# Gated-delta inverse: masks applied as products leave PSUM, blocks gathered and returned by copies with three whole transposes, gate projections regrouped

## The chip, the cores and the metric

One core of a Trainium2 chip runs the whole program once. The time is device microseconds (us) of that execution. TensorE is called PE below, VectorE DVE, ScalarE ACT, GpSimd POOL, the DMA-issuing SyncE SP.

## What is computed

Two blocks of transformer layers on 256 tokens of width 1024, in float32. The first block has two layers (L = 0, 1); each has one input projection, three mixers (state-space, latent attention, gated delta rule), gates and a feed-forward part. The change lies in the gated delta rule, which solves a triangular system per chunk and head:

```python
a_mat = jnp.where(strict, jnp.einsum('bhcld,bhcmd->bhclm', kb, k) * decay, 0.0)
rhs = jnp.concatenate([v * beta[..., None], kb * jnp.exp(g)[..., None]], axis=-1)
sol = lax.linalg.triangular_solve(a_mat + jnp.eye(L, dtype=jnp.float32), rhs, left_side=True, lower=True)
u, w = jnp.split(sol, [DV], axis=-1)
```

The kernel uses chunks of 128 tokens: 2 chunks x 8 heads = 16 triangular matrices of 128x128, each of which it inverts.

## The kernel before

**Streams and order.** Every engine walks the same list of turns (`order1` for a layer of the first block). A turn names a stream (a projection such as `gate_g`, `gate_s`, `xbc`, or a mixer such as `gdn`) and how many of its steps come next; each engine emits its own part of the step. So the list fixes the order on all engines. What PE does in the fill turns covers what the other engines do for `gdn`.

**Projections.** A turn of `gate_g`, `gate_s`, `z`, `lat` or `xbc` is one group of 48 matmuls on PE (lines 912 to 914) from two chunks of weights. A weight chunk arrives by a DMA from SP into a ring of three slots (each two chunks, 1 MB), ACT rounds it to its high part (line 1469, `prepare`), and DVE (line 2103) or POOL (line 2931) subtracts to get the low part; `by_pool` in `rings` picks which. A high slot is free only once PE has used the chunk two groups earlier, so ACT makes the highs of the next group right after the last group ended. For the gate projections ACT then evicts the group (line 1561). `ada0` is a turn of 16 small matmuls (line 871) with a DVE addition (lines 2121, 2124).

**The inverse** (`gdn`, in each engine's class). PE turns (line 837) and ACT negates (line 1772) the 16 matrices into `K.AT`. Then:
- DVE gathers the 16x16 diagonal blocks with four transposes of 32 partitions each (line 2439), puts them into `W` by two predicated copies (line 2444) and inverts them all at once with 28 small operations (`solved`, lines 2432 and 2434). ACT spreads the result (line 1786, four activations) and DVE returns it with eight transposes of 32 partitions (line 2452), four for `K.X`, four for `K.XT`.
- `LEVELS` joins blocks of 16 to 32, 64 and 128, in 12 steps (three levels x four groups of four matrices). A step: POOL masks `AT` into `BT` (line 3022), PE multiplies it by `X` ("y", line 1123), ACT evicts to `Y` (line 1797), PE multiplies by `XT` ("j", line 1131), DVE adds to `XT` (line 2462), PE turns that (line 837) and ACT copies it to `X` (line 1778). On PE, step n is y of the next step, j of this one, the turning of the last one.

Of the kernel before, what the change touches and what calls it, by code (L numbers as in the profile page):

```python
# [153 lines left out]
class Shared:  # L154
# [90 lines left out]
    def rings(self):  # L245
# [3 lines left out]
        for p, (mat, _, c) in enumerate(self.plan()):  # L249
# [4 lines left out]
            self.hi_of[p], self.hi_before[p], self.by_pool[p] = h, at.get(h), mat == "win" and (c < 28 or 52 <= c < 56)  # L254
# [143 lines left out]
    def block1_memory(self):  # L398
# [20 lines left out]
        self.turned, self.W, self.tmp16 = small[:, 0:512], blocks(small[:, 512:768], 16), small[:, 768:832]  # L419
        self.spread = [small[:, 1024 + 512 * i:1536 + 512 * i] for i in range(2)]  # L420
# [135 lines left out]
def order1(L):  # L556
# [18 lines left out]
    yield from [("gdn", 1), ("xbc", 2), ("lat", 1), ("xbc", 1), ("lat", 1), ("gdn", None), ("ssd", 1)]  # L575
# [244 lines left out]
class TensorE(Engine):  # L820
# [243 lines left out]
    def gdn(self, L):  # L1064
# [44 lines left out]
        yield  # L1109
# [8 lines left out]
        def below(lev, q):  # L1118
            P = self.open("gd_y", L, lev, q)
            self.wait_ge(*at("gd_g", "mask", L, lev, q))  # L1120
            self.wait_ge(*(at("gd_s", "X", L, lev - 1, q) if lev > 4 else at("gd_v", "X16", L)))
            for j in range(4):
                i = mm(bank(P, j), K.BT[:, 4 * q + j, :], K.X[:, 4 * q + j, :], True, True)
            i.then_inc(*up("gd_p", "y", L, lev, q))

        def joined(lev, q):
            P = self.open("gd_j", L, lev, q)
            self.wait_ge(*at("gd_s", "Y", L, lev, q))
            self.wait_ge(*(at("gd_v", "XT", L, lev - 1, q) if lev > 4 else at("gd_v", "XT16", L)))
# [326 lines left out]
class ScalarE(Engine):  # L1456
# [291 lines left out]
    def gdn(self, L):  # L1748
# [21 lines left out]
        for c, g in CG:  # L1770
            self.wait_ge(*at("gd_p", "u", L, c, g))
            self.act(K.AT[:, 8 * c + 4 * g:8 * c + 4 * g + 4, :], four(self.bank("gd_u", L, c, g)), ACT.Copy, scale=-1.0).then_inc(*up("gd_s", "A", L, c, g))
            self.emptied("gd_s", "gd_u", L, c, g)
        yield
# [18 lines left out]
        def below(lev, q):  # L1793
# [1449 lines left out]
```

## Time and profile before

| | us |
|---|---|
| median of 3 runs | 2610.51 (2609.53 to 2613.84) |
| the profiled execution | 2610.93 |
| its span | 2609.1 |
| PE busy in the span | 2515.6 (96%) |
| DVE, ACT, POOL busy | 1465.1, 1255.3, 363.5 |

The execution's own time is 1.8 us above its span and 0.4 us above the median of the runs. In the profile, "idle before <-releaser" names what ended an engine's wait, and PEclk is the granted TensorE clock as a share of full speed.

### The profile page before, as it was taken

The numbers are of one execution on the slowest core, as the hardware profiler recorded it, in microseconds if no ns is written. First come the engines' busy times: TensorE is split into PE (matmuls) and PEld (weight loads), VectorE is DVE, ScalarE is ACT, GpSimd is POOL, SyncE is SP. The second block draws the span as 40 slices with busy tenths as digits, with TensorE's granted clock in tenths as the row PEclk, the third lists the DMA queues.
The fourth block names the chain that finished last, engine by engine and source line by source line (L and its number), as shares of the span: only waits on it lengthen the run. The fifth ranks groups of instructions, "written<-read, shape, count | busy, mean of one in ns | idle before, by whom it ended". The sixth has DMA issues, their size and how long they took to land.

```text
span 2609.1 us, 44133 instructions
## 1 busy us (share of the span) xinstructions
PE 2515.6 (96%) x19246; PEld 2326.1 (89%) x19246; DVE 1465.1 (56%) x2212; ACT 1255.3 (48%) x1856; POOL 363.5 (14%) x211
## 2 busy tenths in 40 slices
PE   7989999999999899999999999999999999999999
PEld 7979988999999799979999886787779998888999
DVE  4762865665357547756666337553334554676654
ACT  6635554454366365545644267542223453334442
POOL 5144000000153240000001004300000001331000
PEclk9989999999999899999999999999999999999999
DMA  5334444455543344435554336233334552113455
GB/s 182 131 114 162 146 152 155 162 178 189 185 140 135 114 162 146 162 130 194 175 181 146 109 105 223 82 129 130 145 116 171 199 170 88 67 64 126 165 182 174
DMA packets 56016, 383.90 MB, mean 147 GB/s; under 512 B 6032, under 2 KB 9744, under 8 KB 10000
## 3 DMA queue, kind: packets, MB, share of 16 engines
q1 hardware_dynamic: 55104, 375.90, 41.8%
q10 hardware_dynamic: 720, 5.18, 0.5%
q8 instruction: 152, 2.49, 0.4%
q14 instruction: 40, 0.33, 0.0%
HBM read 380.01 MB, written 1.05 MB: 146 GB/s over the span
## 4 chain that ended last, share of the span: by engine, by line
PE 82%; DVE 10%; ACT 4%; DMA 2%; issue 1%; POOL 0%; DVEq 0%; ACTq 0%; POOLq 0%
PE ps L912 20%; PE ps L914 20%; PE ps L913 20%; DVE r L2103 3%; PE ps L1411 1%; PE ps L1039 1%; PE ps L871 1%; ACT r L1469 1%; PE ps L991 1%; PE ps L993 1%; PE ps L992 1%; PE ps L950 1%; PE ps L951 1%; PE ps L952 1%; PE ps L1131 1%
## 5 line engine op out<-in xcount | busy, mean ns | idle before, releaser
L912 PE MATMUL ps<-r,r 128*128 128x256 f32 (+1 forms) x4512 | 1345.7, 298 | 17.8 <-DVE r L2103 12.2
L914 PE MATMUL ps<-r,r 128*128 128x256 f32 (+1 forms) x4512 | 1332.5, 295 | 0.0
L913 PE MATMUL ps<-r,r 128*128 128x256 f32 (+1 forms) x4512 | 1332.4, 295 | 0.0
L2103 DVE TENSOR_TENSOR r<-ring,r 128x1024 fp32r<-128x1024 f32 (+2 forms) x550 | 668.8, 1250 | 554.8 <-ACT r L1469 554.5
L912 PEld LDWEIGHTS ps<-r,r 128*128 128x128 f32 x4512 | 852.9, 189 | 52.0 <-issue 15.2
L914 PEld LDWEIGHTS ps<-r,r 128*128 128x128 f32 x4512 | 852.3, 189 | 25.0
L913 PEld LDWEIGHTS ps<-r,r 128*128 128x128 f32 x4512 | 852.4, 189 | 24.0 <-issue 0.5
L1469 ACT ACTIVATE r<-ring 128x1024 fp32r<-128x1024 f32 (+1 forms) x614 | 612.5, 1039 | 307.6 <-DMA ring<-in_fi 68.8
L2982 POOL TENSOR_TENSOR slab<-slab 128x512 f32<-128x512 f32 (+1 forms) x20 | 28.7, 1434 | 1296.5 <-ACT slab L1589 1276.1
L2931 POOL TENSOR_TENSOR r<-ring,r 128x1024 fp32r<-128x1024 f32 x64 | 152.5, 2407 | 157.0 <-ACT r L1469 146.8
L2194 DVE SCALAR_TENSOR_TENSOR slab<-ps,v,slab 128x255 f32<-128x255 f32 (+1 forms) x168 | 67.5, 473 | 73.6 <-ACT slab L1541 73.6
L991 PE MATMUL ps<-r,r 128*128 128x256 f32 (+2 forms) x304 | 89.2, 294 | 0.5 <-DVE r L2103 0.4
L992 PE MATMUL ps<-r,r 128*128 128x256 f32 (+2 forms) x304 | 87.4, 288 | 0.0
L993 PE MATMUL ps<-r,r 128*128 128x256 f32 (+2 forms) x304 | 87.4, 287 | 0.0
L950 PE MATMUL ps<-r,r 128*128 128x256 f32 x240 | 72.3, 301 | 10.0 <-DVE r L2278 7.7
L3039 POOL TENSOR_TENSOR slab<-slab,posi 128x1024 f32<-128x1024 f32 (+1 forms) x32 | 46.9, 1468 | 220.8 <-DVE posi L2761 220.8
L1561 ACT ACTIVATE slab<-ps 128x512 f32<-128x512 f32 x48 | 28.5, 594 | 92.8 <-PE ps L914 92.6
L951 PE MATMUL ps<-r,r 128*128 128x256 f32 x240 | 70.2, 292 | 0.0
L952 PE MATMUL ps<-r,r 128*128 128x256 f32 x240 | 70.0, 292 | 0.0
L1610 ACT ACTIVATE r<-slab 128x512 fp32r<-128x512 f32 x33 | 20.8, 632 | 98.4 <-DVE slab L2260 98.4
L3067 POOL TENSOR_TENSOR slab<-slab 128x512 f32<-128x512 f32 x32 | 50.4, 1574 | 102.2 <-PE ps L1411 84.2
L1589 ACT ACTIVATE slab<-x 128x512 f32<-128x512 f32 x36 | 22.7, 631 | 85.7 <-DVE x L2236 52.0
(328 smaller groups left out, 2836.7 us busy)
## 6 DMA issues: line engine op xcount, KB each, us to landing
ring<-in_win SPq DMA_DIRECT2D x76, 1024.0 KB, 4.9
ring<-in_ada SPq DMA_DIRECT2D x48, 1024.0 KB, 4.9
ring<-in_fi SPq DMA_DIRECT2D x44, 1024.0 KB, 4.8
ring<-in_fo SPq DMA_DIRECT2D x36, 1024.0 KB, 4.8
ring<-in_wup SPq DMA_DIRECT2D x32, 1024.0 KB, 4.9
ring<-in_wdn SPq DMA_DIRECT2D x32, 1024.0 KB, 4.8
ring<-in_hin SPq DMA_DIRECT2D x20, 1024.0 KB, 4.8
ring<-in_nqkv SPq DMA_DIRECT2D x12, 1024.0 KB, 4.7
```

The lines of the kernel that those rows point to most:

```text
L912: self.mm(o, hi[:, k - k0, cs], xh, k == 0, False)
L913: self.mm(o, hi[:, k - k0, cs], xl, False, False)
L914: i = self.mm(o, lo[:, k - k0, cs], xh, False, k == last)
L950: self.mm(o, hi, xh, k == 0 and t % per == 0, False, skip_group_check=True)
L951: self.mm(o, hi, xl, False, False, skip_group_check=True)
L952: i = self.mm(o, lo, xh, False, k == kt - 1, skip_group_check=True)
L991: self.mm(o, xh, cut(hi, k), k == 0, False)
L992: self.mm(o, xh, cut(lo, k), False, False)
L993: i = self.mm(o, xl, cut(hi, k), False, k == kt - 1)
L1469: self.act(K.high(p), K.raw(p), ACT.Copy).then_inc(*self.up("w_hi", p))
L2103: self.tt(K.low(p), K.raw(p), K.high(p).bitcast(F32), ALU.subtract).then_inc(*self.up("w_lo_v", p))
L2931: self.tt(K.low(p), K.raw(p), K.high(p).bitcast(F32), ALU.subtract).then_inc(*self.up("w_lo_g", p))
```

## The change

1. `rings`: the low parts of the first four chunks of `gate_s` (52 to 55), two groups, are made by DVE instead of POOL.
2. Gathering: ACT and DVE each copy two of the four diagonal 32-partition strips into one tile, and one transpose of all 128 partitions follows. Return: ACT and DVE each spread one half, one whole transpose for `X` and one for `XT`, and then copies of the strips, two by ACT and two by DVE.
3. Masks: POOL's masking of `AT` is gone. PE multiplies the unmasked `AT`, and DVE multiplies the product by the (transposed) mask as it leaves PSUM; ACT no longer evicts it.
4. `order1`: one more `gate_s` group stands before the first level, one empty step of `gdn` is gone, and an `xbc` turn takes the place of the `gate_s` turn after the levels.
5. A table load before the second half of the output norm is left out, and buffers move.

```diff
@@ rings
-            self.hi_of[p], self.hi_before[p], self.by_pool[p] = h, at.get(h), mat == "win" and (c < 28 or 52 <= c < 56)
+            self.hi_of[p], self.hi_before[p], self.by_pool[p] = h, at.get(h), mat == "win" and c < 28
@@ order1
-    yield from [("gdn", 1), ("gate_g", 1), ("gdn", 1), ("gate_g", 1), ("gdn", 1), ("gate_s", 1), ("gdn", 1), ("gate_s", 1),
-                ("gdn", 1), ("ada0", 1)]
+    yield from [("gdn", 1), ("gate_g", 1), ("gdn", 1), ("gate_g", 1), ("gate_s", 1), ("gdn", 1), ("gate_s", 1),
+                ("gdn", 1), ("gate_s", 1), ("ada0", 1)]
     for _ in range(3):
         yield from [("gdn", 4), ("ada0", 1)]
-    yield from [("gate_s", 1), ("gdn", 1), ("gate_s", 1)]
+    yield from [("gate_s", 1), ("gdn", 1), ("xbc", 1)]
...
-    yield from [("gdn", 1), ("xbc", 2), ("lat", 1), ("xbc", 1), ("lat", 1), ("gdn", None), ("ssd", 1)]
+    yield from [("gdn", 1), ("xbc", 1), ("lat", 1), ("xbc", 1), ("lat", 1), ("gdn", None), ("ssd", 1)]
@@ TensorE.gdn
        def below(lev, q):
-            self.wait_ge(*at("gd_g", "mask", L, lev, q))
-            self.wait_ge(*(at("gd_s", "X", L, lev - 1, q) if lev > 4 else at("gd_v", "X16", L)))
+            if lev > 4:
+                self.wait_ge(*at("gd_s", "X", L, lev - 1, q))
+            else:
+                self.wait_ge(*at("gd_s", "X16", L, 0))
+                self.wait_ge(*at("gd_v", "X16", L, 0))
-                i = mm(bank(P, j), K.BT[:, 4 * q + j, :], K.X[:, 4 * q + j, :], True, True)
+                i = mm(bank(P, j), K.AT[:, 4 * q + j, :], K.X[:, 4 * q + j, :], True, True)
        def joined(lev, q):
-            self.wait_ge(*at("gd_s", "Y", L, lev, q))
+            self.wait_ge(*at("gd_v", "Y", L, lev, q))
@@ ScalarE.gdn
+        for a in quarter[:2]:
+            m = self.act(K.small[a, :].rearrange("p (t x m) -> p t x m", t=16, x=2), K.AT[a, :, a].rearrange("p m (x t) -> p t x m", x=2), ACT.Copy)
...
-            for x in range(2):
-                self.wait_ge(*at("gd_v", "W", L, 14))
-                m = self.act(K.spread[i].rearrange("p (i x m) -> p i x m", i=16, x=2)[:, :, x, :], K.W.rearrange(order), ACT.Copy,
-                             scale=K.upper[x][:, 0, 1:2])
+            self.wait_ge(*at("gd_v", "W", L, 14))
+            self.act(K.spread[i].rearrange("p (i x m) -> p i x m", i=16, x=2)[:, :, 0, :], K.W.rearrange(order), ACT.Copy,
+                     scale=K.upper[0][:, 0, 1:2]).then_inc(*up("gd_s", "spread", L, i))
+        for i, dst in enumerate((K.X, K.XT)):
+            self.wait_ge(*at("gd_v", "back", L, i))
+            for a in quarter[:2]:
+                m = self.act(dst[a, :, a].rearrange("p m (x i) -> p i x m", x=2), K.back[i][a, :].rearrange("p (i x m) -> p i x m", i=16, x=2), ACT.Copy)
-        def below(lev, q):
-            self.act(K.Y[:, 4 * q:4 * q + 4, :], four(self.bank("gd_y", L, lev, q)), ACT.Copy).then_inc(*up("gd_s", "Y", L, lev, q))
@@ VectorE.gdn
-        for a in quarter:
-            self.e.transpose(K.turned[a, :].rearrange("p (t x m) -> p t x m", t=16, x=2),
-                             K.AT[a, :, a].rearrange("p m (x t) -> p t x m", x=2)).then_inc(*up("gd_v"))
+        for a in quarter[2:]:
+            self.e.tensor_copy(K.small[a, :].rearrange("p (t x m) -> p t x m", t=16, x=2), K.AT[a, :, a].rearrange("p m (x t) -> p t x m", x=2)).then_inc(*up("gd_v"))
+        self.e.transpose(K.turned, K.small).then_inc(*up("gd_v"))
...
+        def back(i, order, dst):
+            self.ts(K.spread[i].rearrange("p (i x m) -> p i x m", i=16, x=2)[:, :, 1, :], W.rearrange(order), K.upper[1][:, 0, 1:2], None, ALU.mult).then_inc(*up("gd_v"))
+            self.wait_ge(*at("gd_s", "spread", L, i))
+            self.e.transpose(K.back[i], K.spread[i]).then_inc(*up("gd_v", "back", L, i))
+            for a in quarter[2:]:
+                self.e.tensor_copy(dst[a, :, a].rearrange("p m (x i) -> p i x m", x=2),
+                                   K.back[i][a, :].rearrange("p (i x m) -> p i x m", i=16, x=2)).then_inc(*up("gd_v"))
...
+        def below(lev, q):
+            self.tt(K.Y[:, 4 * q:4 * q + 4, :], four(self.bank("gd_y", L, lev, q)), bc(K.C[f"t{lev}"].unsqueeze(1), [128, 4, 128]),
+                    ALU.mult).then_inc(*up("gd_v", "Y", L, lev, q))
@@ PoolE.gdn
-        def below(lev, q):
-            self.tt(K.BT[:, s4, :], K.AT[:, s4, :], mask(f"t{lev}"), ALU.mult).then_inc(*up("gd_g", "mask", L, lev, q))
```

How instructions now stand. In the changed kernel DVE's lines 2112, 2428, 2441 and 2443 are 2103, 2419, 2432 and 2434 of the kernel before, and ACT's 1478, 1570, 1782 are 1469, 1561, 1772. `r_52` and `r_53` are the two slots of highs, `r_49` to `r_51` the lows.

DVE before, from the last `gdn` step ahead of the inverse to its first operations:

```order
L2419 TENSOR_TENSOR slab<-ps,slab 128x512 x4
L2103 TENSOR_TENSOR r_50<-ring,r_52 128x1024 x2
L2439 STREAM_TRANSPOSE slab<-slab 32x512 x4
L2444 COPY_PREDICATED slab<-cst,slab 128x256 x2
L2432 TENSOR_TENSOR slab<-slab 128x14
```

DVE of the changed kernel at the same place:

```order
L2428 TENSOR_TENSOR slab<-ps,slab 128x512 x4
L2112 TENSOR_TENSOR r_50<-ring,r_52 128x1024 x2
L2112 TENSOR_TENSOR r_51<-ring,r_53 128x1024 x2
L2112 TENSOR_TENSOR r_49<-ring,r_52 128x1024 x2
L2448 COPY slab<-slab 32x512 x2
L2451 STREAM_TRANSPOSE slab<-slab 128x512
L2455 COPY_PREDICATED slab<-cst,slab 128x256 x2
L2441 TENSOR_TENSOR slab<-slab 128x14
```

Two pairs of lows (for the first and second `gate_s` groups) now stand ahead of the gathering; a third pair stands in the middle of the 28 small operations.

ACT of the changed kernel, from the negation to the first turned blocks (before, it was negation, highs in `r_53`, eviction, highs in `r_52`, eviction, then the four activations of line 1786 and an eviction):

```order
L1782 ACTIVATE slab<-ps 128x512 x4
L1788 ACTIVATE slab<-slab 32x512 x2
L1478 ACTIVATE r_53<-ring 128x1024 x2
L1570 ACTIVATE slab<-ps 128x512
L1478 ACTIVATE r_52<-ring 128x1024 x2
L1570 ACTIVATE slab<-ps 128x512
L1478 ACTIVATE r_53<-ring 128x1024 x2
L1570 ACTIVATE slab<-ps 128x512
L1801 ACTIVATE slab<-slab,cst 128x16x16 x2
L1807 ACTIVATE slab<-slab 32x16x2x16 x4
L1570 ACTIVATE slab<-ps 128x512
```

The highs of the second `gate_s` group (`r_52`) stand behind the eviction of the last `gate_g` group, so DVE's second pair of lows, and with it the gathering, comes after that group's end on PE.

DVE of the changed kernel, from the return of `XT` to the first levels (the return of `X`, in the same three rows, stands ahead of it):

```order
L2461 TENSOR_SCALAR slab<-slab,cst 128x16x16
L2464 STREAM_TRANSPOSE slab<-slab 128x512
L2468 COPY slab<-slab 32x16x2x16 x2
L2130 COPY row<-ps 128x256
L2478 TENSOR_TENSOR slab<-ps,cst 128x512 x2
L2490 TENSOR_TENSOR slab<-slab,ps 128x512
L2478 TENSOR_TENSOR slab<-ps,cst 128x512
L2490 TENSOR_TENSOR slab<-slab,ps 128x512
```

The first masked product stands behind both returns and the `ada0` copy, and DVE has two operations per level step where it had one.

## Rows read from the trace of the kernel before

**Rows 1.** The page: busy time by engine, share of the span, instructions.
```profile
PE 2515.6 (96%) x19246; PEld 2326.1 (89%) x19246; DVE 1465.1 (56%) x2212; ACT 1255.3 (48%) x1856; POOL 363.5 (14%) x211
```
**Rows 2.** Waits of PE: engine line waited for, us in total, times, longest.
```profile
PE ps L1123 <- DVE slab L2452: 20.0, 2, 10.0
...
PE ps L1131 <- DVE slab L2452: 1.2, 2, 0.6
```
**Rows 3.** PE's timeline, layer 0: start, us, engine, line, operation, [idle before].
```profile
135.05 0.37 PE L912 MATMUL ps<-r,r 128*128 128x256 f32 x1
...
152.31 1.07 PE L871 MATMUL ps<-ring,silc 128*32 128x256 f32 x16
...
163.40 3.75 PE L1123 MATMUL ps<-slab 128*128 128x128 f32 x16 [10.01 <-DVE slab L2452]
...
173.06 1.06 PE L1123 MATMUL ps<-slab 128*128 128x128 f32 x8
173.96 1.06 PE L1131 MATMUL ps<-slab 128*128 128x128 f32 x8
...
191.91 1.06 PE L1131 MATMUL ps<-slab 128*128 128x128 f32 x8
```
**Rows 4.** PE's timeline, layer 1.
```profile
866.04 3.75 PE L1123 MATMUL ps<-slab 128*128 128x128 f32 x16 [10.03 <-DVE slab L2452]
...
875.95 1.06 PE L1123 MATMUL ps<-slab 128*128 128x128 f32 x8
```
**Rows 5.** Stretches: us of PE, PEld, DVE, ACT, POOL (count), then PEclk, DMA share.
```profile
88.00:90.00 2.00, 2.00 (x12) 2.00 (x11) 1.83 (x6) 0.00 (x0) 0.00 (x0) 0.50 0.00 0
...
165.00:170.00 5.00, 4.42 (x22) 4.16 (x21) 3.13 (x5) 1.20 (x2) 2.55 (x2) 0.50 0.00 0
...
716.00:718.00 2.00, 0.00 (x0) 0.00 (x0) 1.05 (x3) 1.42 (x4) 0.47 (x1) 1.00 0.07 23
```
**Rows 6.** DVE's timeline over the inverse, layer 0.
```profile
143.15 2.25 DVE L2432 TENSOR_TENSOR slab<-slab 128x14 f32<-128x14 f32 x1
...
154.76 0.22 DVE L2432 TENSOR_TENSOR slab<-slab 128x56 f32<-128x56 f32 x1
...
157.84 0.18 DVE L2434 TENSOR_TENSOR slab<-slab 128x14 f32<-128x14 f32 x1
159.00 8.58 DVE L2452 STREAM_TRANSPOSE slab<-slab 32x512 f32<-32x512 f32 x8 [0.97 <-ACT slab L1786]
```
**Rows 7.** POOL's timeline, the same stretch.
```profile
142.65 5.07 POOL L2931 TENSOR_TENSOR r<-ring,r 128x1024 fp32r<-128x1024 f32 x2 [0.73 <-ACT r L1469]
147.67 5.04 POOL L3022 TENSOR_TENSOR slab<-slab,cst 128x512 f32<-128x512 f32 x4
```
**Rows 8.** ACT's timeline, the same stretch.
```profile
141.03 0.60 ACT L1561 ACTIVATE slab<-ps 128x512 f32<-128x512 f32 x1 [3.00 <-PE ps L914]
141.53 2.00 ACT L1469 ACTIVATE r<-ring 128x1024 fp32r<-128x1024 f32 x2
146.72 0.60 ACT L1561 ACTIVATE slab<-ps 128x512 f32<-128x512 f32 x1 [3.20 <-PE ps L914]
```
**Rows 9.** Single lines: count, ns min/median/max.
```profile
L2444 DVE COPY_PREDICATED slab<-cst,slab x4: 647/1072/1496, 140.9 to 845.1; 128x256 f32<-128x256 int32 x4
L2522 DVE TENSOR_SCALAR slab<-slab x16: 426/427/428, 279.6 to 1017.1; 128x512 f32<-128x512 f32 x16
L2462 DVE TENSOR_TENSOR slab<-slab,ps x24: 403/687/689, 169.8 to 898.7; 128x512 f32<-128x512 f32 x16, 64x256 f32<-64x256 f32 x8
```
**Rows 10.** DVE's timeline in the third level, layer 0.
```profile
189.37 2.36 DVE L2103 TENSOR_TENSOR r<-ring,r 128x1024 fp32r<-128x1024 f32 x2 [1.32 <-ACT r L1469]
...
191.98 0.41 DVE L2462 TENSOR_TENSOR slab<-slab,ps 64x256 f32<-64x256 f32 x1
```
**Rows 11.** Two other waits of PE, in its timeline.
```profile
85.56 0.36 PE L912 MATMUL ps<-r,r 128*128 128x256 f32 x1 [2.75 <-DVE r L2103]
...
714.66 1.13 PE L1006 MATMUL ps<-slab,cst 128*128 128x256 f32 x4 [1.70 <-ACT slab L1589]
```

More of the change, by code:

```diff
@@ L418, in block1_memory @@
         small = self.y.rearrange("p a b -> p (a b)")
-        self.turned, self.W, self.tmp16 = small[:, 0:512], blocks(small[:, 512:768], 16), small[:, 768:832]
-        self.spread = [small[:, 1024 + 512 * i:1536 + 512 * i] for i in range(2)]
+        self.small, self.turned = small[:, 0:512], small[:, 512:1024]
+        sums = self.sq.rearrange("p a b -> p (a b)")
+        self.W, self.tmp16 = blocks(sums[:, 0:256], 16), sums[:, 256:320]
+        self.spread = [small[:, 1024 * i:1024 * i + 512] for i in range(2)]
+        self.back = [small[:, 512 + 1024 * i:1024 + 1024 * i] for i in range(2)]
         self.BT = self.rs.rearrange("p a (b c) -> p (a b) c", c=128)
@@ L1676, in squares, with logs @@
         self.act(sq, src, ACT.Square).then_inc(*self.up("n_s", "sq", pid))
-    def logs(self, pid, nt, per, n, inv, rs):
+    def logs(self, pid, nt, per, n, inv, rs, load=True):
         K, groups, pb = self.K, nt // per, 512 // n
-        self.e.preload_act_table_set(LN_EXP)
+        if load:
+            self.e.preload_act_table_set(LN_EXP)
         for g in range(0, groups, pb):
@@ L1773, in gdn @@
             self.emptied("gd_s", "gd_u", L, c, g)
+        quarter = [slice(32 * a, 32 * a + 32) for a in range(4)]
+        self.wait_ge(*mine("gd_s"))
+        for a in quarter[:2]:
+            m = self.act(K.small[a, :].rearrange("p (t x m) -> p t x m", t=16, x=2), K.AT[a, :, a].rearrange("p m (x t) -> p t x m", x=2), ACT.Copy)
+        m.then_inc(*up("gd_s", "small", L))
         yield
@@ L1831, in gdn @@
         for g in range(2):
-            self.logs(("go", L, g), 4, 1, T, 1 / 128, K.rs[:, 4 * g:4 * g + 4, :])
+            self.logs(("go", L, g), 4, 1, T, 1 / 128, K.rs[:, 4 * g:4 * g + 4, :], load=g == 0)
         for g in range(2):
@@ L2434, in solved @@
                 self.tt(W[:, 0:j, j + 1:16], W[:, 0:j, j + 1:16], t, ALU.add).then_inc(*up("gd_v", "W", L, j))
-        for a in quarter:
-            for c, g in CG:
-                self.wait_ge(*at("gd_s", "A", L, c, g))
-            self.e.transpose(K.turned[a, :].rearrange("p (t x m) -> p t x m", t=16, x=2),
-                             K.AT[a, :, a].rearrange("p m (x t) -> p t x m", x=2)).then_inc(*up("gd_v"))
+        for c, g in CG:
+            self.wait_ge(*at("gd_s", "A", L, c, g))
+        for a in quarter[2:]:
+            self.e.tensor_copy(K.small[a, :].rearrange("p (t x m) -> p t x m", t=16, x=2), K.AT[a, :, a].rearrange("p m (x t) -> p t x m", x=2)).then_inc(*up("gd_v"))
+        self.wait_ge(*mine("gd_v"))
+        self.wait_ge(*at("gd_s", "small", L))
+        self.e.transpose(K.turned, K.small).then_inc(*up("gd_v"))
         self.wait_ge(*at("gd_g", "W", L))
@@ L3011, in gdn @@
             self.e.memset(v, 0.0).then_inc(*up("gd_g", "zero", L, i))
[L3012 to L3028 removed]
+        yield
     def na(self):
```

54 lines of the change are left out of this document (22 added, 32 removed).

## The prediction

> **What bounds the kernel now.** I read the page first. PE is busy for 2515.6 of 2609.1 us [rows 1], so only what shortens PE's waits, or what it issues at a lowered clock, can show. The list of PE's waits comes next: two of about 10 us stand out, one in each layer, at the first product of the levels (line 1123), and both end with DVE's return transposes (line 2452); two more of 0.6 us follow at line 1131 [rows 2]. Then PE's timeline around them. In layer 0 PE starts the last `gate_g` group at 135.05, issues it, two `gate_s` groups and `ada0`, has nothing left at 163.40 - 10.01 = 153.39, and goes on at 163.40 [rows 3]; layer 1 shows the same with 10.03 [rows 4]. Last the stretches: the granted clock is 0.50, its 1.2 GHz level, from 165 to 170 with PE nearly always busy [rows 5]. The wait has lowered the clock for the work behind it.
>
> What this costs in all: at full clock a y or a j takes 173.96 - 173.06 = 0.90 us and the turning of four blocks, half as many matmul records, 0.45 by estimate; a step is 2.25. From 163.40 to 173.06 PE issues three y, two j and one turning, 5 x 0.90 + 0.45 = 4.95 at full clock, and takes 9.66 [rows 3]. With 0.58 of that a wait, 4.13 is clock. Layer 1: 875.95 - 866.04 = 9.91 [rows 4], so 4.38 is clock. Together 10.01 + 10.03 + 1.16 + 4.13 + 4.38 = **29.7 us**, the most that the change can win here.
>
> Why DVE is late: its first small operation of the inverse, on 14 elements, takes 2.25 us, and the last, of the same size, 0.18; from 154.76 on 14 of them take 3.26 together [rows 6]. The long ones lie beside POOL's lows and masks, which end at 152.71 [rows 7]. So DVE loses (154.76 - 143.15) - 3.26 = 8.35 us to them. The Trainium skill, SBUF - State Buffer, section "Who interferes with whom", says that a VectorE instruction with two SBUF inputs and a GpSimd instruction that reads SBUF lock each other out; by that rule the loss goes when POOL goes, and the trace agrees with 2.25 against 0.18.
>
> **The change, part by part (layer 0; layer 1 has the same offsets).**
>
> *Cover.* One more `gate_s` group now stands before the first y. A group takes 146.72 - 141.03 = 5.69 [rows 8]. PE is through at 153.39 + 5.69 = 159.08 if nothing stops it. The group is only moved, so its work costs nothing.
>
> *Start of DVE's chain.* DVE must make two pairs of lows before it gathers. The second pair's highs come after the last `gate_g` group: ACT starts them at 141.53 and takes 2.00 [rows 8], so DVE has the first at 142.6 and, at 2.36 for an undisturbed pair [rows 10], is free at 144.95. That is a loss: `AT` is there from about 136.
>
> *Gathering.* Two DVE copies of 32x512 (ACT's two run long before, from 136). The nearest rows: 0.43 for 512 elements by a scalar operation within SBUF, 0.69 out of PSUM [rows 9]; the strided side argues against the lower, so 0.55 each, 1.10. Even a strided strip can hardly exceed the 1.07 of a transpose of it (8.58 / 8) [rows 6]; the low end is 0.43. One transpose of 128x512: 1.07, the row of 32x512, because each partition has as many elements; ends 0.5 and, if strips were done one after another, 4.3. Two predicated copies at 0.65, the fastest seen (the slow 1.50 lay beside POOL) [rows 9]: 1.30. Sum 3.5: 148.45.
>
> *Inverse.* First 14 operations 3.3: 151.75. Then the third pair of lows, first at 152.95, both at 154.1. PE wants the first at 135.05 + 3 x 5.69 + 0.1 = 152.2, so it **waits 0.8** (through a gap that was covered by POOL before) and ends `ada0` (1.08, from 152.31 to 153.39 [rows 3]) at 159.85. Second 14 operations 3.3: 157.4.
>
> *Return.* Scaling on ACT, 0.6, beside DVE's, then the transpose 1.07: 159.15. ACT's two strips 1.2, DVE's 1.1: `X` at 160.45. PE **waits 0.6**. `XT`: DVE scaling 0.35, transpose 1.07, strips 1.1, with gaps 162.9. Then the `ada0` row 0.35 and the first masked product 0.69 (priced by an addition out of PSUM [rows 9]): 163.95. PE has issued two y by 162.25, so it **waits 1.75** for its first j.
>
> *Levels.* DVE now has 0.69 + 0.69 = 1.4 us per step of 2.25, and each masked product is asked for 1.3 us after its y ended. So PE keeps its pace, at one place excepted: in the third level DVE's lows end and its next operation starts at 191.98 [rows 10]. That is now a masked product, ready at about 192.75, and PE wants its j at 191.91 [rows 3]: it **waits 0.85**.
>
> *Costed at nothing:* the two `gate_s` pairs on DVE ahead of the gathering reach PE in time (the first at 139.6 for a group that begins at 140.8); POOL's freed time has no taker; ACT loses evictions and a table load, and PE waits for neither there; the `xbc` group in the place of the `gate_s` one is as long, and its lows (POOL, 4.8 us a pair) have the 5.69 of the `gate_s` group and the products behind the levels as cover. If that cover failed, at most a pair of lows, 4.8, would show. SP's transfers keep their order, only one group nearer.
>
> *Sum.* Waits left 0.8 + 0.6 + 1.75 + 0.85 = 4.0 a layer, 8.0 in all, so 29.7 - 8.0 = **21.7 us gained**, if the clock holds. The profiled execution would take 2610.93 - 21.7 = 2589.2; the median of the runs lies 0.4 lower, and I say 2589.
>
> **The rivals.**
>
> *The clock falls all the same.* A wait of 2.75 [rows 11] was followed by clock 0.50 [rows 5]; one of 1.70 [rows 11] left it at 1.00 even in the idle time after it [rows 5]. Here 0.6 and 1.75 stand 1.8 us apart: between the two. A fall costs between nothing and the 4.13 of now; behind waits a quarter as long I take 2 a layer: 2593. The Trainium skill, TensorE: Matmul & The Clock Gate, section "HAM oscillation", says that waits between bursts lower the clock again and the next burst starts slow; that rule gives this rival, and the trace bears it out for the 2.75 and not for the 1.70.
>
> *DVE's chain is shorter than PE's cover.* With copies at 0.43 and transposes at 0.5, the chain loses 0.7 + 1.1 before `XT` and more with ACT's part; all waits but that of the third level shrink under 1 us: 2582. For it: contiguous transposes. Against: the row.
>
> *Strips are slow.* Copies at 1.07 each: gathering +1.0, each return +1.0, so the waits grow by 3 to 4 a layer, and the clock falls: some 11 less gained: 2600.
>
> *A whole transpose is four strips long* (the other side). 4.3 instead of 1.07 is 3.2 more, three times: waits 0.8 + 0.6 + 1.75 + 0.85 + 9.6 = 13.6, and the clock falls twice as deep into the work, 4.3 as now and 2 behind the wait for the lows: 19.9 a layer against 14.9 now, 10 us slower: 2621 (2610.5 + 10). It decides from 1.6 us more per whole transpose, 2.7 in all. For it: no row has more than 32 partitions. Against: every other DVE row costs by elements per partition.
>
> *POOL was not the cause:* then the first small operations stay long, 8.4 a layer, and the waits with clock come to about 13 of 14.9: 2607. The two rows of one size speak against it.
>
> **How the numbers follow.** Forecast 50%; clock falls 25%; shorter chain 9%; slow strips 9%; long transposes 4%; POOL not the cause 3%. The predicted time is the forecast's, **2589**. From 2581 (all of the 29.7 gained) to 2600 the first four are taken in, with unnamed shifts of PE's phase of a few us. A measurement of this kernel tells about 0.2%, 5 us, from no change. Faster: the first four, 93%. Same: 3% from the last rival. Slower: 4%.
>
> **What would show it.** DVE's small operations all at 0.18 to 0.25 beside an idle POOL; the gathering copies starting near 145; a whole transpose at about 1.07; PE's waits at line 1123 and at the first j of about 0.6 and 1.75, one at the third `gate_s` group of 0.8, and PEclk at 1.00 through the levels. Wrong would be: a wait at line 1123 over 3 us, PE waiting at every j (then DVE's two operations per step are the bound), or `X` ready before PE is.

## The result

The changed kernel takes **2593.7 us**, the median of 4 runs (2591.63 to 2595.91), against 2610.02 (2607.0 to 2613.84) for the kernel before on the same chip: ratio 0.9937, 95% interval 0.992 to 0.9954. It is faster by 16.3 us where 21.7 were forecast; the forecast time was 2589. A second set of runs of the same kernel (`a0_after`) gave 2594.79 and 0.9941 (0.9927 to 0.9954).

| us | before | after |
|---|---|---|
| the profiled execution | 2610.93 | 2595.91 |
| its span | 2609.1 | 2594.1 |
| PE busy | 2515.6 | 2512.4 |
| POOL busy | 363.5 | 312.5 |

The list of PE's waits of the changed kernel, to be held against [rows 2]; the old lines 1123 and 1131 are now 1128 and 1140. Line 1128 is short enough to have left the head of that list: its row is from the groups by line (busy, mean ns, idle before it).

```profile
PE ps L915 <- DVE r L2112: 16.4, 14, 2.8
...
PE ps L1140 <- DVE slab L2478: 2.8, 4, 0.8
```
```profile
L1128 PE MATMUL ps<-slab 128*128 128x128 f32 x192 | 25.6, 278 | 1.8 <-ACT slab L1807 1.8
```

The 21.2 us that both lines waited are 4.6. PE's timeline in layer 0 shows what is left, and one wait that the prediction does not have:

```profile
154.29 0.36 PE L915 MATMUL ps<-r,r 128*128 128x256 f32 x1 [0.55 <-DVE r L2112]
...
162.15 2.02 PE L1128 MATMUL ps<-slab 128*128 128x128 f32 x16 [0.92 <-ACT slab L1807]
164.88 1.16 PE L1140 MATMUL ps<-slab 128*128 128x128 f32 x8 [0.70 <-DVE slab L2478]
...
187.89 1.16 PE L1140 MATMUL ps<-slab 128*128 128x128 f32 x8 [0.78 <-DVE slab L2478]
...
261.42 0.35 PE L915 MATMUL ps<-r,r 128*128 128x256 f32 x1 [2.45 <-DVE r L2112]
```

The first four are the four forecast waits. They make 2.95 us in layer 0 (forecast: 4.0) and 2.68 in layer 1. The stretches (busy us of PE, PEld, DVE, ACT, POOL, then PEclk) say that the clock stays at its 2.4 GHz level in the levels, and is at the 1.2 GHz level behind the last of these waits:

```profile
165.00:170.00 5.00, 5.00 (x46) 5.00 (x47) 3.18 (x5) 0.80 (x2) 0.00 (x0) 1.00 0.37 154
263.00:265.00 2.00, 2.00 (x11) 2.00 (x11) 1.77 (x2) 1.14 (x2) 0.00 (x0) 0.50 0.08 25
```

DVE's timeline over the inverse, against [rows 6]:

```profile
146.25 1.27 DVE L2448 COPY slab<-slab 32x512 f32<-32x512 f32 x2
147.56 0.71 DVE L2451 STREAM_TRANSPOSE slab<-slab 128x512 f32<-128x512 f32 x1
148.37 1.35 DVE L2455 COPY_PREDICATED slab<-cst,slab 128x256 f32<-128x256 int32 x2
149.75 0.17 DVE L2441 TENSOR_TENSOR slab<-slab 128x14 f32<-128x14 f32 x1
...
158.28 0.18 DVE L2443 TENSOR_TENSOR slab<-slab 128x14 f32<-128x14 f32 x1
158.50 0.35 DVE L2461 TENSOR_SCALAR slab<-slab,cst 128x256 f32<-128x256 f32 x1
159.11 0.71 DVE L2464 STREAM_TRANSPOSE slab<-slab 128x512 f32<-128x512 f32 x1 [0.26 <-ACT slab L1801]
159.86 1.27 DVE L2468 COPY slab<-slab 32x512 f32<-32x512 f32 x2
161.17 0.44 DVE L2461 TENSOR_SCALAR slab<-slab,cst 128x256 f32<-128x256 f32 x1
161.64 0.71 DVE L2464 STREAM_TRANSPOSE slab<-slab 128x512 f32<-128x512 f32 x1
162.39 1.26 DVE L2468 COPY slab<-slab 32x512 f32<-32x512 f32 x2
163.67 0.42 DVE L2130 COPY row<-ps 128x256 f32<-128x256 f32 x1
164.13 1.29 DVE L2478 TENSOR_TENSOR slab<-ps,cst 128x512 f32<-128x512 f32 x2
```

The first small operation takes 0.17 where it took 2.25. A whole transpose of 128 partitions takes 0.71, less than the transpose of one strided strip of 32 did (8.58 / 8 = 1.07 [rows 6]). From the last small operation to the first y pass 162.15 - 158.28 = 3.9 us; before it was 163.40 - 157.84 = 5.6 [rows 3, 6].

**Where the time went.** The runs of one kernel scatter by 4 us and more, the timeline of the changed part by tenths. So I read every profile also by two stretches of each layer, between rows of PE that all kernels have: S1 from the first Gram product (line 1090 of the kernel before) to the first product with the finished inverse (line 1149), S2 from there to the first product of the state-space part (line 1231). Each is cut into stretches of 2 us: "idle" is the length less PE's busy time, "clock" the busy time times (1 - PEclk), "work" the rest.

| both layers, us | before | after | difference |
|---|---|---|---|
| S1 idle | 21.20 | 6.15 | -15.05 |
| S1 clock | 8.52 | 0 | -8.52 |
| S2 idle | 4.91 | 7.04 | +2.13 |
| S2 clock | 0 | 3.18 | +3.18 |
| S1 and S2, work | 427.03 | 428.63 | +1.60 |
| S1 and S2, length | 461.66 | 445.00 | -16.66 |

So the part with the inverse gave 23.6 us, more than was forecast, and 5.3 came back in S2 as a wait and a lower clock. (One group of weights has moved from S2 to S1, so work is read for both together.) All that lies outside these stretches is 2147.4 us before and 2149.1 after; over the 14 profiles of this study it is 2145.8 to 2155.7, mostly by the clock in places that the change does not touch.

### The profile page after: what moved, and what is told of

It reads as the page before. It is cut to its first block, busy times and chain, and to the rows that moved or that the text cites. A ratio compares the mean times of both kernels' runs of the same rounds, so it can differ in the third digit from the quotient of the medians.

```text
span 2594.1 us, 44101 instructions
## 1 busy us (share of the span) xinstructions
PE 2512.4 (97%) x19246; PEld 2321.4 (89%) x19246; DVE 1460.9 (56%) x2242; ACT 1250.7 (48%) x1838; POOL 312.5 (12%) x179
## 4 chain that ended last, share of the span: by engine, by line
PE 82%; DVE 9%; ACT 5%; DMA 2%; issue 1%; POOL 0%; DVEq 0%; POOLq 0%; ACTq 0%
PE ps L915 21%; PE ps L916 20%; PE ps L917 20%; DVE r L2112 3%; PE ps L1042 1%; PE ps L1420 1%; ACT r L1478 1%; PE ps L874 1%; PE ps L994 1%; PE ps L996 1%; PE ps L995 1%; PE ps L840 1%; PE ps L1367 1%; PE ps L953 1%; PE ps L955 1%
## 5 line engine op out<-in xcount | busy, mean ns | idle before, releaser
L2112 DVE TENSOR_TENSOR r<-ring,r 128x1024 fp32r<-128x1024 f32 (+2 forms) x558 | 678.6, 1250 | 557.6 <-ACT r L1478 557.4
L2959 POOL TENSOR_TENSOR r<-ring,r 128x1024 fp32r<-128x1024 f32 x56 | 132.7, 2390 | 231.6 <-ACT r L1478 221.7
```

Of the source, the lines that this page charges most:

```text
L2112: self.tt(K.low(p), K.raw(p), K.high(p).bitcast(F32), ALU.subtract).then_inc(*self.up("w_lo_v", p))
L2959: self.tt(K.low(p), K.raw(p), K.high(p).bitcast(F32), ALU.subtract).then_inc(*self.up("w_lo_g", p))
```

## The experiments

My theory after the result: the missing 5.4 us are the new wait in front of the second `lat` group in each layer, with its fall of the clock, and the order of the groups makes it. Rivals: the lows that DVE took over from POOL hold the inverse up, and: the gain itself is not owed to what I put it down to. All ratios are to the kernel before on the same chip; "S" is the length of S1 and S2 of both layers in the run's profile.

| run | median | ratio (95%) | S |
|---|---|---|---|
| before | 2609.7 to 2611.9 | | 461.7 |
| the change (first result) | 2593.7 | 0.9937 (0.992 to 0.9954) | 445.0 |
| `a0_after` | 2594.79 | 0.9941 (0.9927 to 0.9954) | 443.2 |
| `e1_lat_first` | 2595.56 | 0.9943 (0.993 to 0.9955) | 447.7 |
| `e2_early_gather` | 2593.31 | 0.9935 (0.9923 to 0.9948) | 443.6 |
| `e3_pool_lows` | 2598.44 | 0.9954 (0.9937 to 0.9971) | 446.4 |
| `b1_dve_lows` | 2605.91 | 0.9987 (0.9975 to 1.0) | 455.1 |
| `b2_order` | 2608.69 | 0.9994 (0.9983 to 1.0005) | 458.7 |
| `b3_order_dve_lows` | 2611.54 | 1.0002 (0.9992 to 1.0011) | 459.3 |
| `c2_strips` | 2612.15 | 1.0001 (0.9992 to 1.0011) | 458.4 |
| `c3_pool_masks` | 2594.54 | 0.9942 (0.9929 to 0.9956) | 442.7 |
| `a1_ada` | 2595.68 | 0.994 (0.9927 to 0.9952) | 442.3 |
| `e5_two` | 2594.4 | 0.9936 (0.9923 to 0.9948) | 446.3 |
| `e4_mix` | 2589.4 | 0.992 (0.9905 to 0.9935) | 438.9 |

### The new wait: can the order take it away?

`a0_after` is the changed kernel itself, to be compared with.

> The changed kernel as it is, beside its variants on one chip. All theories: about 2594 us, some 16 us under the kernel before; it is the mark for the other runs of this call.

`e1_lat_first` puts the first `lat` turn ahead of the last two `xbc` turns.

```diff
-    yield from [("gdn", 1), ("xbc", 1), ("lat", 1), ("xbc", 1), ("lat", 1), ("gdn", None), ("ssd", 1)]
+    yield from [("gdn", 1), ("lat", 1), ("xbc", 1), ("xbc", 1), ("lat", 1), ("gdn", None), ("ssd", 1)]
```

> The changed kernel with the turn of lat ahead of the turn of xbc behind the gdn turn that holds the sums of the output norm, so that ACT makes the highs of the second lat group before it evicts the last xbc group. Theory A (5 us of the forecast gain went into a new wait of 2.45 us a layer for the lows of the second lat group, and a fall of the clock behind it): that wait and the fall go, 2 x (2.45 + 1.75) = 8.4 us less, about 2585. Rival B (the missing gain is scatter of the clock falls from other waits, and the lat wait is neutral because it also stood in the kernel before with 1.4 us): within 3 us of the changed kernel, 2591 to 2594.

It gained nothing. The wait of 2.45 us is gone, and two groups later, in the state-space part, a longer one stands. PE's timeline, and the row of ACT's behind which the highs of that group are queued (they start at 272.22, DVE's lows at 273.29):

```profile
274.66 0.36 PE L915 MATMUL ps<-r,r 128*128 128x256 f32 x1 [3.38 <-DVE r L2112]
```
```profile
271.69 0.63 ACT L1859 ACTIVATE slab<-slab 128x512 f32<-128x512 f32 x1 [0.85 <-DVE slab L2550]
```

The clock falls behind it too. S2 is 122.8 us a layer instead of 120.2 to 121.5. The theory had the place right and the remedy wrong. In the changed kernel ACT works through this list between the norm of the inverse's output and the lows of the second `lat` group (ACT's timeline, and DVE's lows behind it):

```profile
253.97 2.15 ACT L1700 ACTIVATE slab<-slab 128x1024 f32<-128x1024 f32 x2
256.03 0.82 ACT L1550 ACTIVATE slab<-ps,v 128x256 f32<-128x256 f32 x2
256.87 1.28 ACT L1563 ACT_TABLE_LOAD   x1
258.16 0.91 ACT L1563 ACTIVATE slab<-slab,v 128x256 f32<-128x256 f32 x2
258.98 1.99 ACT L1478 ACTIVATE r<-ring 128x1024 fp32r<-128x1024 f32 x2
```
```profile
260.05 2.36 DVE L2112 TENSOR_TENSOR r<-ring,r 128x1024 fp32r<-128x1024 f32 x2 [0.74 <-ACT r L1478]
```

The roots, the eviction and silu of `xbc` with a table load, then the highs. The kernel before has the same work there, with one pair of highs straight behind the roots, at 260.70. What differs more is PE. Behind the statistics of that norm, before the state-space part, it had three groups to issue and now has two; the third is the `xbc` group that now stands right behind the levels. ACT and DVE are the chain there, and this reordering within the stretch only chose in front of which group PE waits. That the order makes the wait is shown further down by `b2_order`, which has the new order and nothing else of the change.

`a1_ada` therefore brings cover from earlier in S2: the second of the two adaptation products (`ada0`) that stand among the `xbc` groups, 1.07 us of PE with hardly any ACT work. The two expectations that call it the product of the levels have its place wrong: on PE it starts at 233.52 in the changed kernel, where the inverse is finished at 198.7, and at 258.12 in this run.

```diff
-        if n in (0, 2):
+        if n == 0:
             yield ("ada0", 1)
-    yield from [("gdn", 1), ("xbc", 1), ("lat", 1), ("xbc", 1), ("lat", 1), ("gdn", None), ("ssd", 1)]
+    yield from [("gdn", 1), ("xbc", 1), ("lat", 1), ("ada0", 1), ("xbc", 1), ("lat", 1), ("gdn", None), ("ssd", 1)]
```

> The changed kernel with one thing altered: the adaptation product of the levels (1.07 us of PE) stands between the two latent groups. If its place there covers the wait of 2.45 us by its own length and keeps the clock up: 1.07 + up to 1.5 us of clock a layer, less nothing in the levels, 2590 to 2592. If the product was cover where it stood, the levels get a new wait of up to 1.07 us and it stays at 2594 to 2595.

No wait came where the product had stood, and S1, which the edit does not touch, is 100.5 and 100.4. The wait fell from 2.45 to 1.51, another of 1.7 came in the state-space part, and the clock stayed at 1.00 through S2 in both layers: S is 442.3, 2.7 less than in the first profile of the change and 0.9 less than in that of `a0_after`, where the clock had fallen in one layer only. The run's median does not show it: its profile has 2155.7 us outside the stretches, the most of all. On the median alone the expected 2590 to 2592 was missed, and the edit's worth is read from S2 only.

### The inverse: what brought the gain?

`e3_pool_lows` gives POOL its two pairs of lows back.

```diff
-            self.hi_of[p], self.hi_before[p], self.by_pool[p] = h, at.get(h), mat == "win" and c < 28
+            self.hi_of[p], self.hi_before[p], self.by_pool[p] = h, at.get(h), mat == "win" and (c < 28 or 52 <= c < 56)
```

> The changed kernel with the lows of the first two gate_s groups made by POOL again. Theory A (lock between POOL's and DVE's reads): the small operations beside POOL take 1 to 2.4 us again, but DVE starts its chain about 5 us earlier because no lows stand ahead of it; X comes within 2 us of where it comes now, and the time is within 3 us of the changed kernel. Rival D (POOL was never what slowed them, the order and the transposes were): small operations at 0.2 us throughout, DVE's chain 5 us shorter, waits at the first y gone, 2590 or less.

2598.4 against 2594.8 for `a0_after`, 3.6 more where at most 3 were expected, with intervals of the ratios that overlap, and 3.2 us more in S (1.4 more than in the first profile of the change). DVE's, POOL's and PE's timelines:

```profile
139.50 3.38 DVE L2455 COPY_PREDICATED slab<-cst,slab 128x256 f32<-128x256 int32 x2
142.91 2.26 DVE L2441 TENSOR_TENSOR slab<-slab 128x14 f32<-128x14 f32 x1
...
147.55 2.33 DVE L2441 TENSOR_TENSOR slab<-slab 128x26 f32<-128x26 f32 x1
149.91 0.19 DVE L2443 TENSOR_TENSOR slab<-slab 128x26 f32<-128x26 f32 x1
```
```profile
139.74 10.10 POOL L2959 TENSOR_TENSOR r<-ring,r 128x1024 fp32r<-128x1024 f32 x4 [7.06 <-ACT r L1478]
```
```profile
142.43 0.39 PE L915 MATMUL ps<-r,r 128*128 128x256 f32 x1 [1.30 <-POOL r L2959]
```

While POOL subtracts, a DVE operation of 26 elements takes 2.33 us, and the next one of the same size takes 0.19, an instant after POOL's end at 149.84. This repeats [rows 6, 7] and agrees with what the Trainium skill, SBUF - State Buffer, section "Who interferes with whom", says of the two engines. But it costs little: counted from the first Gram product, DVE gathers after 40.5 us instead of 48.7 in `a0_after`, and loses that lead, and 1.2 us more, beside POOL (last small operation after 61.9 us, 60.7 in `a0_after`). PE also waits for POOL's lows themselves, 1.30 and 1.33 us in the two layers, and no longer in front of the third `gate_s` group. In all, S1 has 2.0 us more of idle time than in `a0_after`; the other difference is a fall of the clock in S2, 1.7 us, that `a0_after` did not have in one of the layers. With the copies in place, taking the lows away from POOL is for the most part a trade of one for the other.

The same was then tried on the kernel before: the lows alone, the order alone (with one more `gdn` turn, which the old streams need), and both.

The first hunk is in `b1_dve_lows` and `b3_order_dve_lows`, the other in `b2_order` and `b3_order_dve_lows`.

```diff
@@ rings
-            self.hi_of[p], self.hi_before[p], self.by_pool[p] = h, at.get(h), mat == "win" and (c < 28 or 52 <= c < 56)
+            self.hi_of[p], self.hi_before[p], self.by_pool[p] = h, at.get(h), mat == "win" and c < 28
@@ order1
-    yield from [("gdn", 1), ("gate_g", 1), ("gdn", 1), ("gate_g", 1), ("gdn", 1), ("gate_s", 1), ("gdn", 1), ("gate_s", 1),
-                ("gdn", 1), ("ada0", 1)]
+    yield from [("gdn", 1), ("gate_g", 1), ("gdn", 1), ("gate_g", 1), ("gate_s", 1), ("gdn", 1), ("gate_s", 1),
+                ("gdn", 1), ("gate_s", 1), ("gdn", 1), ("ada0", 1)]
...
-    yield from [("gate_s", 1), ("gdn", 1), ("gate_s", 1)]
+    yield from [("gate_s", 1), ("gdn", 1), ("xbc", 1)]
...
-    yield from [("gdn", 1), ("xbc", 2), ("lat", 1), ("xbc", 1), ("lat", 1), ("gdn", None), ("ssd", 1)]
+    yield from [("gdn", 1), ("xbc", 1), ("lat", 1), ("xbc", 1), ("lat", 1), ("gdn", None), ("ssd", 1)]
```

> The kernel before with the two pairs of lows of the gate_s groups moved from POOL to DVE, nothing else. Theory P (the 8.35 us that DVE loses beside POOL simply come back): the first y is no more than about 2 us late in each layer and its clock fall goes, so 20 to 25 us less, 2587 to 2592. Theory T (a trade: DVE gathers only after two pairs of lows, at 145.0 instead of 136.3, and then runs alone: strips 4.56, predicated 1.3, 28 small operations 6.6, so it ends at 157.5 where it now ends at 158.0): the wait stays at 9.5 us with its clock fall, within 3 us of before.

> The kernel before with the new order of the groups alone (POOL's lows and masks, strips by transposes kept). If the moved group is pure cover: 5.7 us less wait a layer, 11 us in all, 2599 or less. If the moved group's own lows come into DVE's chain (2.4 us) and the later wait at the second latent group appears (1.1 us more wait and 1.5 us of clock a layer, as in the changed kernel), what is left is 5.7 - 2.4 - 2.6 = 0.7 a layer: 2607 to 2612.

> Order and lows on DVE together, without the copies, whole transposes and masked products: the changed kernel less its new gathering. If these three bring nothing of their own, it is within 2 us of the changed kernel, 2595. If they are what shortens the chain (strips 4.56 before against copies and one transpose 2.0, and 5.4 us from the last small operation to the first y against 3.7, and masks off POOL), a wait of about 5 us stays at the first y in each layer and the clock still falls behind it: 2604 to 2609.

None comes near the changed kernel. `b1_dve_lows` wins 6.6 us in S and some 4 us in the median, at the edge of its interval: more than the trade foretold, far less than the 20 to 25 of the other theory. Its PE no longer waits 10 us in one place but in three (PE's timeline), and the clock falls behind the first and the last:

```profile
150.64 0.58 PE L912 MATMUL ps<-r,r 128*128 128x256 f32 x1 [4.25 <-DVE r L2103]
...
160.45 2.02 PE L1123 MATMUL ps<-slab 128*128 128x128 f32 x16 [0.83 <-DVE slab L2452]
...
164.80 1.55 PE L1131 MATMUL ps<-slab 128*128 128x128 f32 x8 [2.33 <-DVE slab L2452]
```

The times of `b2_order` and `b3_order_dve_lows` cannot be told from those of the kernel before, though their profiles have 3.0 and 2.4 us less in S. The moved group, which I had counted as 5.69 us of cover a layer, does cover something: in `b2_order` S1 has 7.6 us less idle time than before and 2.2 less of clock, both layers together. But S2 gives it back, 3.8 of idle time and 3.4 of clock, with one long wait in front of the second `lat` group, where the kernel before waits 0.35 and 1.03 us (PE's timeline):

```profile
269.18 0.36 PE L912 MATMUL ps<-r,r 128*128 128x256 f32 x1 [3.29 <-DVE r L2103]
```

So the order alone makes the new wait. This is the second theory on record for `b2_order` (2607 to 2612, measured 2608.69), with a dearer wait than it foretold. In `b3_order_dve_lows`, 2.5 us above its range, the 6.6 us that the lows win in the old order do not come on top.

`c2_strips` and `c3_pool_masks` then split what remains. `c2_strips` is the changed kernel with gathering and return by transposes of single strips; the copies of strips by ACT and DVE go, and ACT spreads both halves, as in the kernel before:

```diff
@@ DVE, gathering
-        self.e.transpose(K.turned, K.small).then_inc(*up("gd_v"))
+        for a in quarter:
+            self.e.transpose(K.turned[a, :].rearrange("p (t x m) -> p t x m", t=16, x=2), K.AT[a, :, a].rearrange("p m (x t) -> p t x m", x=2)).then_inc(*up("gd_v"))
@@ DVE, back
-            self.e.transpose(K.back[i], K.spread[i]).then_inc(*up("gd_v", "back", L, i))
...
+            for a in quarter:
+                self.e.transpose(dst[a, :, a].rearrange("p m (x i) -> p i x m", x=2),
+                                 K.spread[i][a, :].rearrange("p (i x m) -> p i x m", i=16, x=2)).then_inc(*up("gd_v"))
```

> The changed kernel with gathering and return by transposes of single strips, as before the change; lows on DVE, order and masked products stay. From the rows: gathering 4.5 us of strips (b3_order_dve_lows) against two copies and one transpose 2.0, so 2.5 later at the inverse; return 0.2 + 0.98 + 4.3 to the first y against 3.7, so 1.7 later. If the copies are what the change lives on, the first y waits about 5 us and the first j over 2, the clock falls behind them, and it is 7 to 8 us a layer worse than the changed kernel: 2607 to 2611, near b3_order_dve_lows. If the masks off POOL matter as much, it lies in the middle, near 2602.

`c3_pool_masks` keeps the copies and undoes the masked products: POOL masks `AT` into `BT` again, PE multiplies that, and ACT evicts y.

```diff
-                i = mm(bank(P, j), K.AT[:, 4 * q + j, :], K.X[:, 4 * q + j, :], True, True)
+                i = mm(bank(P, j), K.BT[:, 4 * q + j, :], K.X[:, 4 * q + j, :], True, True)
@@ DVE
-            self.tt(K.Y[:, 4 * q:4 * q + 4, :], four(self.bank("gd_y", L, lev, q)), bc(K.C[f"t{lev}"].unsqueeze(1), [128, 4, 128]),
-                    ALU.mult).then_inc(*up("gd_v", "Y", L, lev, q))
@@ ACT
+            self.act(K.Y[:, 4 * q:4 * q + 4, :], four(self.bank("gd_y", L, lev, q)), ACT.Copy).then_inc(*up("gd_s", "Y", L, lev, q))
@@ POOL
+            self.tt(K.BT[:, s4, :], K.AT[:, s4, :], mask(f"t{lev}"), ALU.mult).then_inc(*up("gd_g", "mask", L, lev, q))
```

> The changed kernel with the masks as before the change: POOL masks the inputs, PE multiplies the masked copy, ACT takes the products out of PSUM. Copies, whole transposes, order and lows on DVE stay; it is the counterpart of c2_strips. In b3_order_dve_lows POOL's four first masks take 7.0 us from 134.7 to 141.7 and only the first pair of lows lies beside them (3.5 us where 2.4 is the rule), well before DVE gathers. If the copies and whole transposes alone are what the change lives on, this run is as fast as the changed kernel, 2592 to 2597, its first j even earlier (ACT takes the first product instead of DVE), and the two stretches of the layers sum to 443 to 446 us. If the masked products are a part of the gain, the first y or the levels wait some 3 us a layer more, with clock: 2601 to 2606.

Without the copies and whole transposes, but with everything else of the change, the times show no gain (2612.2, ratio 1.0001; S is 3.3 us shorter than before); without the masked products, but with the copies, there is all of it (2594.5, S 442.7). So the copies are needed and the masked products are not. Whether the copies would bring the 16 us in the old order too is not shown: every run that has them has the new order. PE's timeline of `c2_strips`, then DVE's:

```profile
156.65 0.53 PE L915 MATMUL ps<-r,r 128*128 128x256 f32 x1 [2.98 <-DVE r L2100]
...
166.35 2.02 PE L1127 MATMUL ps<-slab 128*128 128x128 f32 x16 [1.25 <-DVE slab L2448]
...
171.83 1.13 PE L1138 MATMUL ps<-slab 128*128 128x128 f32 x8 [3.46 <-DVE slab L2458]
```
```profile
146.16 4.50 DVE L2436 STREAM_TRANSPOSE slab<-slab 32x512 f32<-32x512 f32 x4
```

and PE's of `c3_pool_masks`, whose first j waits 0.7 us longer than in the changed kernel, since ACT evicts y only after its strips; in exchange the wait of 0.78 in the third level, which DVE's masked product had made, is gone:

```profile
162.27 2.02 PE L1129 MATMUL ps<-slab 128*128 128x128 f32 x16 [1.07 <-ACT slab L1808]
165.71 1.16 PE L1141 MATMUL ps<-slab 128*128 128x128 f32 x8 [1.41 <-ACT slab L1817]
```

The gathering is 4.50 us of DVE with strips, and 1.27 + 0.71 with two copies and the whole transpose, the other two copies being ACT's, ahead of time. The return costs DVE 8.72 with strips, and 0.35 + 0.71 + 1.27 and again 0.44 + 0.71 + 1.26 = 4.74 without. So 2.5 + 4.0 = 6.5 us less on the engine that is late; the 2.5 and half of the 4.0, the return of `X`, lie before the first y.

These runs also price the fifth part of the change. Idle time in S2 is 4.4 us a layer in `b2_order` and `b3_order_dve_lows` and 3.5 in the changed kernel, in `c2_strips` and in `c3_pool_masks`. Neither the copies nor the masks can make that difference, so by elimination it is the table load that ACT no longer does in the output norm (1.28 us), or the moved buffers; no run undoes it alone.

### A version that beats both

`e2_early_gather` is `e1_lat_first` with DVE's gathering one `gdn` step earlier, ahead of the second pair of lows.

```diff
+        self.e.transpose(K.turned, K.small).then_inc(*up("gd_v"))
         yield
...
-        self.e.transpose(K.turned, K.small).then_inc(*up("gd_v"))
```

The waits and copies that lead up to that transpose move with it.

> As the last one, and DVE gathers and transposes the diagonal blocks one gdn step earlier, ahead of both pairs of lows, while it is idle. Theory A (DVE's chain to X and XT, held up by the lows ahead of it, sets the waits 0.55, 0.92 and 0.70 in each layer): the chain is 2.1 us shorter, at least 2.0 of the 2.2 us go, 4 us less than the last one, about 2581. Rival C (the ACT copies of 1.1 us each, or the third pair of lows in the middle, set them): they stay over 0.5 each, less than 2 us gained.

S1 fell from 101.7 and 100.3 in `e1_lat_first` to 98.8 and 98.1, its idle time from 6.1 to 1.8 us: all waits of the inverse are gone but the one in the third level. The total missed the expectation by 12 us for the reason above, the wait of 3.38 in each layer and the clock behind it, which `e1_lat_first` had brought.

`e4_mix` joins that gathering with the change's own order of the last groups and the moved product of `a1_ada`; `e5_two` moves a second product there too. Its expectation takes that for the one ahead of the first y, but the edit moves the other one from among the `xbc` groups (on PE from 213.69 to 253.07), and the one ahead of the first y stays, at 158.35. So what was expected of S1 was not tested.

> The changed kernel with DVE's gathering one step earlier (as in e2_early_gather), its own order of the last groups (not that of e1), and the adaptation product that stood in the levels (1.07 us of PE, hardly any of ACT) put between the two latent groups, where PE waits 2.45 us. If the wait there is ACT's chain and any work of PE covers it: it shrinks to 1.4, and its clock fall (1.5 us a layer) goes: 2 us a layer less than e2_early_gather in that stretch and no new wait in the levels, 2588 to 2590. If the wait only moves on (as in e1), it is found again at the first groups of the state-space part: 2593.

> e4_mix with the adaptation product ahead of the first y put there too, two in all between the latent groups. X is ready about 0.5 us after PE would now ask for it (158.5 against 158.0 in e4_mix), so about 0.5 us a layer is won on balance: 2588.5. If a third limit stands close behind (DMA of the next chunk, which ACT waited 1.5 us for in e4_mix), nothing is won: 2589.5 to 2590.5.

`e4_mix` is the fastest: 2589.4 us (2587.5 to 2595.02), ratio 0.992 (0.9905 to 0.9935), 22.8 us less in S than the kernel before and 4 to 6 less than the change. Its interval still overlaps that of the change, so against the change it rests on S. Two waits of 1.5 and 1.6 (1.7 in layer 1) are left in S2, and PEclk is 1.00 in all of S1 and S2, in both layers:

```profile
256.61 0.36 PE L915 MATMUL ps<-r,r 128*128 128x256 f32 x1 [1.51 <-DVE r L2112]
...
271.62 0.36 PE L915 MATMUL ps<-r,r 128*128 128x256 f32 x1 [1.61 <-DVE r L2112]
```

`e5_two` overdid it: 2594.4, and S 7.5 higher. S1 is unchanged, since nothing in it was moved, but in S2 one wait of 5.55 stands in the place of the two, and the clock falls behind it. PE's timeline, then ACT's:

```profile
260.56 0.55 PE L913 MATMUL ps<-r,r 128*128 128x256 f32 x1 [5.55 <-DVE r L2110]
```
```profile
258.10 2.00 ACT L1476 ACTIVATE r<-ring 128x1024 fp32r<-128x1024 f32 x2 [4.31 <-DMA ring<-in_win]
```

I expected at worst no gain. The third limit that the expectation names is what the trace shows: ACT waits 4.31 us for the chunk of weights, where it waited 1.52 in `e4_mix`. SP issues it at 253.17, when PE is through with the group before, and it lands at 258.07; the two places in the ring that came free before that, at 238.32 and 244.02, went to the weights of the two moved products. A moved step brings its DMA and its place in the ring with it.

## Why the prediction was right, and where it was not

*What bounds the kernel, the ceiling of 29.7.* Right. The two stretches give the terms back: 21.20 idle and 8.52 clock in S1, all of the clock returned.

*POOL beside DVE, 8.35 us a layer.* The fact was right, the weight was not. The operations shrank as forecast, but `e3_pool_lows` puts POOL back and loses 1.4 to 3.2 us in both layers together, and `b1_dve_lows` wins 6.6 where twice 8.35 were lost to POOL. The sum escaped the error because it also charged the later start of the gathering (144.95; measured 146.25, as DVE's second pair began at 143.86 behind ACT's two strips of 1.13).

*Gathering 3.5.* Measured 148.37 + 1.35 - 146.25 = 3.5. Two errors cancel: copies 0.64 instead of 0.55, the whole transpose 0.71 instead of 1.07. Here the row decided wrongly. It was a row of strided strips of 32 partitions, and no run tells whether the stride or something else made it dearer. The 0.53, my estimate from the Trainium skill, Vector Engine (DVE) Microarchitecture Reference, section 3.8, lies nearer to 0.71 than the 1.07 does. For 512 contiguous elements per partition the measured 0.71 is what counts.

*The four waits.* Forecast 0.8, 0.6, 1.75, 0.85; measured 0.55, 0.92, 0.70, 0.78 in layer 0. The first y waits for ACT, whose strips were put at 0.6 each and take 1.1:

```profile
159.86 2.19 ACT L1807 ACTIVATE slab<-slab 32x512 f32<-32x512 f32 x2 [0.21 <-DVE slab L2464]
162.38 2.20 ACT L1807 ACTIVATE slab<-slab 32x512 f32<-32x512 f32 x2 [0.33 <-DVE slab L2464]
```

The first j came 1 us better, by the two short transposes. Left were 5.6 in both layers instead of 8.0.

*Cover, 5.69 for nothing.* Half true. The group covers (S1 of `b2_order`: 7.6 us of idle time and 2.2 of clock less in both layers), but not for nothing: the same run pays 7.3 us for it in S2.

*Masks as products.* I gave them no gain of their own, but held the masks on POOL for a part of DVE's loss. `c3_pool_masks` shows that they could have stayed: it is as fast, and the forecast wait of 0.85 in the third level (0.78 measured) was the price of the masked product alone.

***"Costed at nothing: the `xbc` group in the place of the `gate_s` one".*** **This is the step that failed.** The time lies in the range all the same, because this step cost only some 5 us net. I asked whether its lows would be ready where it goes and not what was left behind where it came from. There ACT's chain behind the output norm had three groups of cover and now has two, and `b2_order`, with the order alone, has the wait. Price: 2.13 of waiting and 3.18 of clock in the first profile. With 1.60 of added work in the table that is 6.9 against the 1.9 by which the inverse did better, a net 5.0 of the missing 5.4. The table load was costed at nothing in the same line; by the elimination above PE would wait some 0.9 us a layer longer there if ACT still did it.

*The rivals.* The clock did fall, but not where that rival had it; its 2593 is near the result by accident. The shorter chain was half true (the transposes at 0.71). Slow strips hold for ACT's copies, 1.1 each, and cost 0.3 us. Long transposes and an innocent POOL are excluded by the rows.

## What to carry to other kernels

Ask of a moved piece of cover what it covered where it stood: a chain on another engine that runs alongside does not show as a wait until its cover is gone. A loss that is seen in the trace (DVE beside POOL) is not yet a gain when it is removed; undo the parts one by one, for here the 16 us hang on one part, the copies with whole transposes, and all the others together brought nothing without it that the times show. Undoing a part says that it is needed, not that it would be enough. And read where a run gains and where it loses: `b2_order` looks like no change and is a gain of 10 us beside a loss of 7. Where a few us are at stake among runs that scatter by as much, measure between two rows that all versions have.

## What the runs showed of the hardware

- A DVE transpose of 128 partitions with contiguous rows of 512 elements takes 0.71 us; one of a strided strip of 32 partitions takes 1.12 (4.50 for four); a DVE copy of such a strip 0.64, ACT's 1.13.
- The same wait does not always lower the clock. The one of 2.45 or 2.46 us in front of the second `lat` group stands in both layers of the change's two profiles and of those of `e3_pool_lows`, `c2_strips` and `c3_pool_masks`: the clock fell behind it in 7 of these 10 cases, for 1.4 to 1.7 us. It fell behind all four waits of 3.38 (`e1_lat_first`, `e2_early_gather`) and all four of 3.3 (`b2_order`, `b3_order_dve_lows`), and behind none of the pairs of 1.5 to 1.7 (`a1_ada`, `e4_mix`).
- The last long run of groups, 1536 matmuls with PE always busy and PEclk 1.00, takes 179.1 to 179.2 us in seven of the 14 profiles (116.7 ns from one matmul to the next) and 180.9 us (117.8 ns) in the other seven, `a0_after` and the first profile of the change among them. That is 1.7 us for the same PE instructions. What sets it stayed open.
